# The wait for an expert's down matrix stands in the chunk loop, and Pool's small first loads wait for the first weight unit

## What is computed

```python
def moe_tokens(x, w_router, r_bias, wg, wu, wd):
    ...                      # the two best experts of a token, and their weights "combine"
    h = jax.nn.silu(jnp.einsum('td,edf->tef', x, wg)) * jnp.einsum('td,edf->tef', x, wu)
    h = h * combine[..., None].astype(h.dtype)
    return jnp.einsum('tef,efd->td', h, wd)
```

## Time and profile before

| | us |
|---|---|
| median of 3 runs | 1327.65 (1323.92 to 1329.11) |
| the profiled execution, its own time | 1324.23 |
| span of the profiled execution | 1322.6 |
| PE busy | 1139.5 (86% of the span) |
| DVE, ACT, POOL busy | 417.7, 265.4, 226.4 |
| TensorE's mean granted clock | 0.948 of full speed |
| moved by DMA | 360.33 MB, mean 272 GB/s |

### The profile page before, as it was taken

One profiled execution on the slowest core, in us unless ns is written; L12 is line 12 of the kernel. 1 busy time (PEld: TensorE's weight loads), 2 busy tenths in 40 slices (PEclk: granted clock), 3 DMA queues, 4 the chain that ended last, 5 costly groups with the idle time before them and its releaser, 6 DMA issues.

```text
span 1322.6 us, 27256 instructions
## 1 busy us (share of the span) xinstructions
PE 1139.5 (86%) x10768; PEld 746.4 (56%) x10769; DVE 417.7 (32%) x1149; ACT 265.4 (20%) x541; POOL 226.4 (17%) x399
## 2 busy tenths in 40 slices
PE   6998788999999879998868999989998799988850
PEld 4676545575776645554435776657765455555520
DVE  0026562713142452221112301522522622222216
ACT  1013732112230321111101302111411411111101
POOL 2003995000000001322212100000000012222222
PEclk9999997999999979998888999999999799999976
DMA  9746779943359729799999800715779197999972
GB/s 323 273 128 194 236 247 325 388 165 123 132 219 384 311 107 423 302 403 422 425 423 383 307 0 27 296 40 214 255 284 401 47 399 306 400 389 393 423 304 75
DMA packets 102625, 360.33 MB, mean 272 GB/s; under 512 B 9639, under 2 KB 11703, under 8 KB 94362
## 3 DMA queue, kind: packets, MB, share of 16 engines
q1 hardware_dynamic: 89986, 332.68, 65.7%
q0 software_dynamic: 12432, 26.51, 5.7%
q10 hardware_dynamic: 144, 0.28, 0.1%
HBM read 341.48 MB, written 18.38 MB: 272 GB/s over the span
## 4 chain that ended last, share of the span: by engine, by line
PE 58%; DMA 19%; DVE 10%; issue 7%; ACT 3%; SPq 1%; POOLq 1%; POOL 1%; DVEq 0%; ACTq 0%
PE acc L733 37%; DMA by_slot<-feats 10%; PE psS L733 8%; DMA ring<-in_w_exp_down 5%; PE psV L733 4%; PE psN L733 3%; DVE feats L1468 2%; DMA feats<-in_w_exp_down 2%; PE acc L1039 2%; PE acc L848 1%; DMA ring<-in_w_in_even 1%; DMA arena<-by_slot,arena 1%; PE psN L1157 1%; ACT arena L1346 1%; ACT feats L2148 1%
## 5 line engine op out<-in xcount | busy, mean ns | idle before, releaser
L733 PE MATMUL acc<-feats,ring 128*128 128x288 f32 x1280 | 315.7, 409 | 10.5 <-ACT feats L2057 4.2
L733 PEld LDWEIGHTS acc<-feats,ring 128*128 128x128 f32 x1280 | 244.7, 192 | 80.2 <-issue 9.5
L2272 POOL DMA_DIRECT2D by_slot<-feats x208 | 103.8, 499 | 524.6 <-DVE feats L1881 321.9
L733 PE MATMUL psS<-ring,feats 128*32 128x256 f32 x2176 | 138.8, 412 | 40.1 <-issue 38.8
L733 PEld LDWEIGHTS psS<-ring,feats 128*32 128x32 f32 x2176 | 74.8, 119 | 93.8 <-issue 56.0
L733 PE MATMUL psS<-arena,feats 128*32 128x256 f32 x1408 | 88.9, 402 | 22.6 <-issue 22.0
L2158 ACT ACTIVATE feats<-psS 64x256 f32<-64x256 f32 x52 | 19.6, 377 | 333.5 <-PE psS L733 333.5
L1346 ACT ACTIVATE arena<-acc 128x1024 f32<-128x1024 f32 (+6 forms) x86 | 65.4, 781 | 103.3 <-PE acc L733 34.7
L733 PE MATMUL psN<-arena,feats 128*32 128x256 f32 (+1 forms) x1360 | 83.5, 379 | 1.5 <-DVE feats L1800 1.5
L1873 DVE TENSOR_TENSOR feats<-feats,psS 64x256 f32<-64x256 f32 x52 | 22.1, 425 | 195.2 <-ACT feats L2158 194.3
L733 PEld LDWEIGHTS psS<-arena,feats 128*32 128x32 f32 x1408 | 45.7, 115 | 55.7 <-issue 31.7
(11 more groups left out here) (344 smaller groups left out, 1224.3 us busy)
## 6 DMA issues: line engine op xcount, KB each, us to landing
ring<-in_w_exp_gate SPq DMA_DIRECT2D x22, 2048.0 KB, 15.1
ring<-in_w_exp_up SPq DMA_DIRECT2D x22, 2048.0 KB, 16.2
ring<-in_w_exp_down SPq DMA_DIRECT2D x22, 2048.0 KB, 24.2
arena<-in_w_exp_gate SPq DMA_DIRECT2D x10, 2048.0 KB, 15.1
arena<-in_w_exp_up SPq DMA_DIRECT2D x10, 2048.0 KB, 19.5
feats<-in_w_exp_down SPq DMA_DIRECT2D x10, 2048.0 KB, 23.8
ring<-in_cache_k SPq DMA_DIRECT2D x64, 256.0 KB, 3.2
ring<-in_cache_v SPq DMA_DIRECT2D x64, 256.0 KB, 3.1
```

Source lines behind the costliest of these rows:

```text
L733: return pe.matmul(out, lhsT, rhs, start=first, stop=last)
L2272: pool.dma_start(by_slot[rows, 256 * q:256 * q + 256], YS[32 * q:32 * q + 32, at]).then_inc(S.stored, 16)
```

## The change

The wait for an expert's matrices is split. In front of the expert PE now waits for gate and up only, and the wait for down stands in the chunk loop, in front of the down products, so it is passed once in each chunk (the value waited for is the same in all chunks of an expert). And Pool waits for unit 0 to land before it issues its first small load.

```diff
@@ experts(l), on PE
-                    W = []
+                    W, arrival = [], []
                     for j in range(3):
                         where, landed, before = place(l, p, j)
                         W.append(where.rearrange("p (k n) -> p k n", k=(8, 8, 4)[j]))
-                        pe.wait_ge(landed, before + 16 + (0 if n is None else 16 * (n + (p == 0))))
+                        arrival.append((landed, before + 16 + (0 if n is None else 16 * (n + (p == 0)))))
+                    for j in range(2):
+                        pe.wait_ge(*arrival[j])
...
                         pick(S, c + 1)
                         turn_h(S, c)
                         turn_picked(S, c + 1)
+                        pe.wait_ge(*arrival[2])
                         down(S, c, W[2])
@@ on Pool
         def _(pool):
+            arrived(pool, 0)
             pool.dma_start(prow[0:6, :], ln_g.rearrange("l k d -> (l k) d")).then_inc(in_rows, 16)
```

## The result

| | before | changed | ratio, with its 95% interval |
|---|---|---|---|
| median of 6 executions each | 1325.28 us | 1309.49 us | 0.9876 (0.9856 to 0.9897) |
| lowest to highest | 1323.92 to 1329.11 | 1305.93 to 1314.53 | |
| profiled execution | 1324.23 us, span 1322.6 | 1307.01 us, span 1305.4 | |

The forecast was 1314.0 us. By the ratio the changed kernel stands at 1308.9 us, just outside the low end of 1309. The ratio is not quite the quotient of the two medians (that is 0.9881), so a gain has two readings here, 15.8 us by the medians and 16.4 by the ratio; the text says which it uses.

What follows compares the result with a forecast made beforehand. Bound by weight loads: PE waits for unit 0 at the start and for down at each block's last expert. 5.1 + 5.3 + 3.7 - 0.4 = 13.7 us off 1327.65 gives 1314.0 us, range 1309 to 1321.

Steps and rivals of the forecast that it cites:

- The start: At the kernel's start, PE's first product comes 3.7 us earlier without Pool's loads beside unit 0; bounds 3.1 to 4.7.
- the tokens' own gain: At the start, the tokens land earlier without Pool's first loads beside them: 0.6 us taken, 1.6 at the most.
- The new bound: At the start, the last token tile's copy, at 16.68 us, bounds PE's first product instead of unit 0's landing.
- landing of the table: Pool's delayed table load lands near 33 to 36 us, before DVE reads it at 72.35, so the delay costs nothing.
- The experts: At each block's last expert, products start after up lands, not down, gaining 5.1 us in block 0, 5.3 in block 1.
- The wait: In the chunk loop, the added wait for down, passed 52 times, costs 0.4 us net; bounds -1.3 to 2.1.
- The clock: The last experts' gate and up products keep their durations, 6.26 and 6.40 us, with 1 us either way per block.
- Case (c): Rival: PE's clock stays at 2.4 GHz before the last experts, 5.3 us more gained, 1308.7 us; chance 0.07.
- Passed on: Behind both blocks the experts' gain passes on, with 1.6 us of slack left at Pool's last store in block 1.
- Case (a): Rival: a later stage swallows the start's gain, 1317.7 us, or half the experts' gain is lost, 1319.2; chance 0.17.
- the last term of the range: An allowance in the whole kernel's forecast range for the median of few runs, about 2 us.
- The sum's terms: Over the whole kernel, gains at the start and both blocks' last experts, less the added wait: 5.1 + 5.3 + 3.7 - 0.4 = 13.7 us.

Runs made afterwards that it cites:

- Pool alone: The kernel before with only Pool's small loads held back until unit 0 has landed, the wait for down left in front of the expert: 1322.99 us, ratio 0.9982.
- the wait for the tokens: The kernel before with one edit, Pool's small loads waiting until the tokens have landed, the experts' waits as before: 1321.18 us, ratio 0.9965.
- down loaded first: The changed kernel with SP issuing each expert's matrices in the order down, gate, up instead of gate, up, down: 1319.21 us, ratio 0.9936 to the kernel before.
- the five waits: The changed kernel with the added wait for down in the chunk loop written five times instead of once: 1314.36 us, ratio 0.9914 to the kernel before.
- Four comparisons: The changed kernel measured four times against the kernel before: medians 1309.49, 1315.38, 1312.38 and 1311.84 us, ratios 0.9876, 0.9915, 0.9898 and 0.9900.
- the waits in the loop: The changed kernel with the waits for gate and up moved into the chunk loop too, behind the table reads: 1310.65 us, ratio 0.9850 to the kernel before.
- fourth measurement: The changed kernel, unaltered, measured a fourth time against the kernel before: 1311.84 us, ratio 0.9900.

## Why the prediction was right in its mechanism and short in its size

- **The start, 3.7 us.** It was 4.2, 3.9 and 4.2 us in the changed kernel, with Pool alone and with the wait for the tokens, 4.1 on the mean. The term that I had taken too small is the tokens' own gain: they start PE at 7.92 instead of 9.31, 1.4 us and not 0.6. Part of that is chance, since the two other executions without a wait on Pool have 8.65 and 8.64, so some 1.0 us is the better number. The new bound is ACT's copy of the last token tile, as forecast. Unit 0 came still earlier than I had it, at 12.98 instead of 14.9 to 15.9: Pool's loads had held it up by 6.6 us, not by the 3.7 to 4.7 of their own bytes and packets. Behind the tokens this is worth nothing. The landing of the table at 29.5 was sooner than my 33 to 36.
- **The experts, 5.1 and 5.3 us.** Up lands 5.4 and 5.3 us before down, and PE starts 1.75 us after it. The table of last landings gives 5.9 and 4.8, and with down loaded first the old distance from the last landing to the last product is back. The step holds.
- **The wait, -0.4 us.** The one wait costs nothing that can be seen, and by the five waits some 0.01 us per chunk. The bounds (0.04 for a hop, 0.16 for the gap between experts) were both above that; the 0.82 us of the gap is not five equal shares. What fills it besides waits are the table reads and the loop's entry: with both ahead of the waits the start follows the landing by 0.14 us.
- **The clock.** The last experts' products ran at the mixed level again (4.99 and 6.23 us behind 5.27 and 5.94 us of idle; the granted clock from 1263.5 to 1269.5 us is 0.58). Case (c) didn't come. It came nearest at the expert before the last in block 1: its idle fell from 7.81 to 2.76 us, but its products still took 5.35 us, where 3.66 had followed 2.21 us of idle in the earlier trace rows. In block 0 the products took 4.99 us and not the 6.26 "as now"; that 1.3 us lies a little outside the 1 us allowed, and the unchanged kernel has 5.35 in its second execution.
- **Passed on.** Behind block 0 the filling products and the norm's chain meet again with 0.80 us of idle, 16.3 us earlier than in the earlier trace rows. Behind block 1 Pool's store followed with 0.98 us of slack. Case (a) didn't come.
- **The step that failed is the last term of the range**, "about 2 us for the median of few runs". The 1327.65 that the sum was taken from, a median of three, became 1325.28 with six: 2.4 us. The gain of this one comparison was 2.1 us above the sum: together 4.5 where 2 were allowed. Four comparisons give single gains from 11.3 to 16.4 us and medians of before from 1325.28 to 1329.01 (the last from the run with the waits in the loop), so the term had to be 3 to 4 us on each side. Nor does the range hold its own bounds when they fall on one side: 1314.0 - 1.0 (start) - 2 (clock) - 1.7 (wait) - 2 (median) is 1307.3, and it ended at 1309.
- **The sum's terms** were each some 0.4 us too small by the rows: the start 4.1 for 3.7, the experts 10.8 for 10.4, the wait next to nothing for -0.4. That makes 14.9 and not 13.7, so that the 13.6 of the four ratios comes so near to the sum is in part luck. The row that I took as typical, 6.26 us of products and 10.71 to the end, was the slowest of its kind; the same kernel again took 9.26.

Open stays what makes the granted clock fall to 0.91 in one execution of the same code from 100 to 300 us and not in the other; no run here shows it, only that this is where the profiled executions of those two measurements part. Also open is the rest between the terms as read from the rows (4.1 + 10.8 = 14.9) and the totals (13.6 by the ratios, 14.2 by the medians); it is smaller than what one comparison can tell.

## What to carry to other kernels

A wait for several transfers in front of a loop should be taken apart by the operation that reads each of them; it costs next to nothing here and gives back the time between the landings, once for every stretch in which the loads set the pace and PE then goes on alone, not once for every expert. The same idea goes further: dividing the transfer that is waited for gave another 8 to 9 us, and reading the loop bounds and entering the loop before the wait took 1.6 us off each restart. And where executions differ by 0.5% in places that the edit doesn't touch, test a theory on an interval between two events of one trace that encloses only the edit.

## What the hardware showed that I had not expected

- A wait on a semaphore that is already set takes PE some 0.01 us: thirteen chunks took 105.14 us with five waits in each and 104.65 with one.
- Two reads of the table into PE's registers and the entry into the loop together keep PE from its next product for 1.6 us (1.75 with them behind the landing, 0.14 with them ahead), while in a stretch without late transfers the whole gap is 0.80 us.
- Pool's 1.43 MB delayed a 2 MB load of SP's queue by more than their own bytes take: unit 0 landed at 12.98 without them and at 19.62 with them, 6.6 us, where 1.43 MB are 3.7 us at the 382 GB/s of the earlier trace rows.
- In four executions, all of the last two measurements, ACT and DVE both stood for 2 to 3 us in the last chunk of block 0 with their input ready, released by nothing that the trace names; in the changed kernel's fourth execution it happened in block 1 too. Timeline of ACT and of DVE of the changed kernel, fourth measurement:

```profile
700.30 0.38 ACT L2151 ACTIVATE feats<-psN 128x256 f32<-128x256 f32 x1 [2.58 <-remote]
```

```profile
700.35 0.29 DVE L1878 COPY feats<-psV 128x128 f32<-128x128 f32 x1 [2.17 <-remote]
```

In the earlier executions this copy waits 0.92 us for PE. I have no cause for it; it is why those executions are not in the table of last landings.
